# A decoder layer's kernel written anew around other layouts of its input, queries and keys

## The reference

```python
h = rmsnorm(x, norm_w)                              # x: 1024 tokens x 2048, float32
qa, ka, va, ga, qb, kb, vb, gb = split(h @ w_in)    # 1024 1024 1024 1024 1024 128 128 1024
qa, ka = rope(rmsnorm(qa)), rope(rmsnorm(ka))       # per head of 64 columns; 8 heads x 2 maps
p = softmax(causal(qa @ ka.T / 8))                  # two maps per head
oa = (p[map 0] - lam * p[map 1]) @ va               # 8 heads, values 128 wide
ya = rmsnorm(oa, subln_w) * (1 - lam_init) * silu(ga)
qb, kb = rope(rmsnorm(qb)), rope(rmsnorm(kb))       # 16 query heads, 2 key heads
p = softmax([window_128(qb @ kb.T / 8), sink])[..., :-1]
yb = (p @ vb) * silu(gb)
out = x + concat(ya, yb) @ w_out                    # 2048 x 2048
```

## Time and profile before

| | |
|---|---|
| median of three runs | 1878.39 us |
| the profiled execution | 1879.02 us |
| its span in the trace | 1877.2 us |
| TensorE busy | 1807.0 us, 96% |
| DVE, ACT, POOL busy | 59%, 43%, 23% |
| mean granted clock of TensorE | 0.993 |
| HBM traffic | 138.71 MB read, 45.09 MB written |

### The profile page before, as it was taken

How to read it: one execution, slowest core, us unless ns; L and a number is a source line. 1 busy time by engine, 2 the same in 40 slices (tenths; PEclk the granted TensorE clock), 3 DMA queues, 4 the chain that set the end, 5 groups by cost and what they waited for, 6 DMA issues and landing times.

```text
span 1877.2 us, 27880 instructions
## 1 busy us (share of the span) xinstructions
PE 1807.0 (96%) x8920; PEld 1507.0 (80%) x8920; DVE 1109.2 (59%) x2255; ACT 799.8 (43%) x2116; POOL 439.0 (23%) x664
## 2 busy tenths in 40 slices
PE   3899999999999999999999999999999889999999
PEld 3788878888788887888878888888888678788887
DVE  5734465665656657566575666758677866333333
ACT  5411354444544445444444444445444554222221
POOL 6512131322313223131231312313223521000000
PEclk9999999999999999999999999999999889999999
DMA  5122222222222222222222222323323544444445
GB/s 201 36 79 73 84 72 78 78 78 78 71 77 77 77 78 71 85 69 87 68 74 86 73 84 74 105 82 83 109 80 98 189 127 122 162 154 161 142 143 177
DMA packets 256504, 184.97 MB, mean 99 GB/s; under 512 B 31136, under 2 KB 227744, under 8 KB 255392
## 3 DMA queue, kind: packets, MB, share of 16 engines
q1 hardware_dynamic: 254352, 183.85, 32.3%
q10 hardware_dynamic: 2064, 0.01, 0.1%
HBM read 138.71 MB, written 45.09 MB: 98 GB/s over the span
## 4 chain that ended last, share of the span: by engine, by line
PE 79%; DVE 9%; issue 4%; DMA 3%; ACT 2%; POOL 2%; SPq 1%; DVEq 0%; ACTq 0%
PE ps_a L854 19%; PE ps_a L856 19%; PE ps_a L855 19%; PE ps_b L938 3%; PE ps_b L856 3%; PE ps_b L854 3%; PE ps_b L855 3%; PE ps_a L898 2%; DVE stage_rows L1124 2%; DMA qkv_sb<-qkv_a_dram 2%; PE ps_a L897 2%; PE ps_b L953 2%; PE ps_b L891 2%; PE ps_b L984 1%; DVE w_lo_sb L1124 1%
## 5 line engine op out<-in xcount | busy, mean ns | idle before, releaser
L854 PE MATMUL ps_a<-hT_hi,w_hi_sb 128*128 128x512 f32 x1696 | 694.1, 409 | 7.2 <-DVE stage_rows L1208 4.5
L856 PE MATMUL ps_a<-hT_hi,w_lo_sb 128*128 128x512 f32 x1696 | 667.4, 394 | 0.0
L855 PE MATMUL ps_a<-hT_lo,w_hi_sb 128*128 128x512 f32 x1696 | 664.1, 392 | 0.0
L1124 DVE TENSOR_TENSOR w_lo_sb<-w_raw_sb,w_hi_sb 128x512 fp32r<-128x512 f32 (+1 forms) x320 | 228.3, 716 | 272.1 <-ACT w_hi_sb L657 270.1
L856 PEld LDWEIGHTS ps_a<-hT_hi,w_lo_sb 128*128 128x128 f32 x1696 | 320.1, 189 | 71.8
L854 PEld LDWEIGHTS ps_a<-hT_hi,w_hi_sb 128*128 128x128 f32 x1696 | 321.2, 189 | 70.2 <-issue 7.2
L855 PEld LDWEIGHTS ps_a<-hT_lo,w_hi_sb 128*128 128x128 f32 x1696 | 321.8, 190 | 58.5
L657 ACT ACTIVATE w_hi_sb<-w_raw_sb 128x512 fp32r<-128x512 f32 (+1 forms) x320 | 197.8, 620 | 226.4 <-DMA w_raw_sb<-in_w_out 95.0
L817 ACT ACTIVATE expd<-ps_a,neg_max 128x256 f32<-128x256 f32 (+7 forms) x128 | 95.1, 743 | 213.3 <-DVE neg_max L1265 211.4
L749 ACT ACTIVATE attention_parts<-ps_b 128x512 fp32r<-128x512 f32 (+3 forms) x160 | 76.9, 521 | 224.2 <-PE ps_b L938 224.0
L1124 DVE TENSOR_TENSOR ps_a<-ps_a,mask 128x128 f32<-128x128 f32 (+2 forms) x192 | 77.5, 417 | 142.2 <-PE ps_a L898 140.8
(11 more groups left out here) (126 smaller groups left out, 2651.6 us busy)
## 6 DMA issues: line engine op xcount, KB each, us to landing
w_raw_sb<-in_w_in SPq DMA_DIRECT2D x200, 256.0 KB, 3.1
w_raw_sb<-in_w_out SPq DMA_DIRECT2D x104, 256.0 KB, 3.1
qkv_a_dram<-stage_rows SPq DMA_DIRECT2D x48, 256.0 KB, 2.4
qkv_sb<-qkv_a_dram SPq DMA_DIRECT2D x64, 192.0 KB, 3.0
x_raw_sb<-in_x SPq DMA_DIRECT2D x8, 1024.0 KB, 7.6
gates_dram<-stage_rows SPq DMA_DIRECT2D x32, 256.0 KB, 2.7
gate_y<-gates_dram SPq DMA_DIRECT2D x128, 64.0 KB, 2.4
y_dram<-gate_y SPq DMA_DIRECT2D x128, 64.0 KB, 2.3
```

The source lines that it names most:

```text
L854: pe.matmul(dst, a_hi, b_hi, start=start, stop=False)
L855: pe.matmul(dst, a_hi, b_lo, start=False, stop=False)
L856: return pe.matmul(dst, a_lo, b_hi, start=False, stop=stop)
L1124: return dve.tensor_tensor(o, a, b, op)
```

## The change

The program is new; the arithmetic of the projections, of the attention and of the output is the same, with the same three matmuls for each product.

- The host hands over the input twice, as it is and transposed (`in_xT`), and the weights with their columns and rows in the order in which tiles are read. PE transposes no input. Channel block k of xT is 128x1024; ACT scales it by `norm_w` into `hT_hi`, DVE makes `hT_lo`. The token factor 1/rms is left out of it: the sums of squares come from x as it is (`square_rows`), and the factor is applied to values and gates later, and cancels for queries and keys but for EPS, which is scaled with it.
- The first 4 tiles (pairs 0 and 1) are computed together while the input arrives, in 16 units of 24 matmuls. Then the values are computed with tokens as rows, in 48 units of 24 matmuls that are 384 wide. Then come 37 tiles in half quarters: 296 slots of 12 matmuls 128x512. The weight tiles pass through rings of two raw and three split ones.
- Columns of queries and keys are ordered so that a tile holds the first halves of four heads, and its partner the second halves. Each such pair of tiles is normalised and rotated as it lies, in two jobs of 512 tokens: squares (ACT), their sum (POOL), a matmul with a matrix of 1/64 that sums over a head's rows (`sum_squares`, L865 and L866, 52 matmuls in all), Ln and Exp(-0.5 ln) on ACT, a Newton step (DVE), products with the tables (POOL) and with the head (DVE), hi and lo. There are 26 jobs, two of them for the B keys. Queries and keys are stored as hi and lo, and are read in the form in which the scores need them, so a step transposes and splits neither.
- A step of A takes 2 slots for i < 4 and 4 slots for i >= 4; a step of B takes 3 slots. Its parts stand in later slots by the numbers of `Step`.
- Gates are the last 16 tiles. y and gates are stored apart; `prep` reads both back, POOL multiplies, ACT and DVE split. Four of the 32 pieces stand in the last slots, 28 in the first 14 units of the output, two each.
- All code is written out; there is no loop on the chip.

```diff
-            def turn_tile(d, b, n, bank):
-                wait(pe, pp_copied[b], d["T"] + 1)
-                bank_free(n)
-                for r in range(4):
-                    mm = pe.transpose(p_tr[bank][:, r * P:(r + 1) * P], stage[:, b, r * P:(r + 1) * P], ident[:, :])
-                mm.then_inc(sm["tp_done"], 1)
-            def turn_qk(nk, i, it, first):
...
-                for a in range(2 if nk == "A" else 3):
-                    mm = pe.transpose(bank[:, a * P:(a + 1) * P], qkv[:, i % 2, a * P:(a + 1) * P], ident[:, :])
+def stage_slots(j):
+    pr, d = divmod(j, 2)
...
+    e = 8 * pair_tiles(pr)[1] + 6 + d + (pr == KB_PAIR)
+    h = e + d
+    return dict(sq=e, hl=h + 1, ss=h + 2, u=h + 3, ln=h + 3, nw=h + 4, p1=h + 5, p2=h + 6, out=h + 7, st=h + 8)
+class Step:
...
+        if self.a:
+            wide = self.i >= 4
+            self.s1 = x + 2 if wide else x
+            self.tp = self.s1 + 2
+            self.pv = self.tp + (2 if wide else 1)
+            self.sq, self.osc, self.to = self.pv + 1, self.pv + 2, self.pv + 3
+            self.after = x + (4 if wide else 2)
+        else:
+            self.tp, self.pv = x + 3, x + 5
+            self.after = x + 3
+            def load_xT(k):
+                wait(sp, x_lo, k - 3)
+                sp.dma_start(xT_sb[k % 4], xT[k * P:(k + 1) * P, :]).then_inc(xT_in[k % 4], 16)
+            def load_rows(r):
+                wait(sp, x_sq, r - 1)
+                sp.dma_start(x_rows[r % 2], x[r * P:(r + 1) * P, :]).then_inc(xr_in[r % 2], 16)
+            for k in range(4, KT):
+                load_w(k)
+                load_xT(k)
+                if k < 4 + NR:
+                    load_rows(k - 4)
```

On ACT the start, and the part of a job with Ln and Exp:

```diff
+            def split_w(u):
...
+                act.wait_ge(w_in[u % 2], 16 * (u // 2 + 1))
+                wait(act, w_used, u - 2)
+                act.activation(w_hi[:, u % 3, 0:w], w_raw[:, u % 2, 0:w], ACT.Copy).then_inc(w_hi_ready, 1)
+            for k in range(KT):
+                act.wait_ge(xT_in[k % 4], 16 * (k // 4 + 1))
+                act.activation(hT_hi[:, k, :], xT_sb[k % 4], ACT.Copy, scale=pars[:, C_NORM + k:C_NORM + k + 1])\
+                    .then_inc(x_hi, 1)
+                split_w(k)
+                if 6 <= k < 6 + NR:
+                    square_rows(k - 6)
+            def job_ln(j):
+                d = j % 2
+                act.wait_ge(u_ready, j + 1)
+                act.activation(bufY[d], bufX[d], ACT.Ln).then_inc(ln_done, 1)
+                act.wait_ge(ln_done, j + 1)
+                act.activation(bufQ[d], bufY[d], ACT.Exp, scale=-0.5).then_inc(y0_done, 1)
+                act.wait_ge(y0_done, j + 1)
+                act.activation(bufY[d], bufQ[d], ACT.Square).then_inc(y0_sq, 1)
```

On DVE the walk through the slots, in which a new weight tile stands first and the jobs' parts stand behind the attention's, but for `job_u`:

```diff
+            for slot in range(-48, NHS + 1):
+                if slot < 0:
+                    split_w(U_V + slot + 48 + 2)
+                elif slot % 2 == 0 and slot < NHS:
+                    split_w(U_T + slot // 2 + 2)
...
+                for j in jobs_at("u", slot):
+                    job_u(j)
...
+                for j in jobs_at("nw", slot):
+                    job_newton(j)
+                for j in jobs_at("p1", slot):
+                    job_prod1(j)
...
```

On POOL the product of y and gate:

```diff
+            def prep_mul(j):
+                half, k = prep_hk(j)
+                t = slice(half * 512, (half + 1) * 512)
+                pool.wait_ge(y_in[j % 5], 32 * (j // 5 + 1))
+                pool.tensor_tensor(g_ring[j % 5], f(hT_lo[:, k, t]), g_ring[j % 5], ALU.mult).then_inc(y_mul, 1)
```

More of the change, by code:

```diff
@@ new lines, with steps_at @@
+FIRST_HS = 4
+STEPS = []
+for _g in range(AH * NR + NB * NR):
+    STEPS.append(Step(_g, STEPS[-1].after if STEPS else FIRST_HS))
+NS = len(STEPS)
+def steps_at(what, hs):
+    return [st for st in STEPS if {"s0": st.s0, "s1": st.s1, "tp": st.tp, "pv": st.pv, "to": st.to,
+                                   "sq": st.sq, "osc": st.osc}[what] == hs]
+USE = {}
+for _hs in range(NHS + 16):
+    for _st in steps_at("tp", _hs):
+        for _m in range(len(_st.spans)):
+            USE["P", _st.g, _m] = len(USE)
+    for _st in steps_at("to", _hs):
+        USE["O", _st.g] = len(USE)
@@ L702, in evacuate @@
-            def evacuate(d, before, u, it, first):
-                for b in range(2):
-                    wait(act, sm["w_used" if b else "pp_done"], u * 4 + 4 if b else u + 1)
-                    stage_free(before, b, it, first)
-                    if d["turned"]:
-                        act.activation(stage[:, b, :], p_proj[b], ACT.Copy).then_inc(pp_copied[b], 1)
-                    else:
-                        act.activation(stage[:, b, :], p_proj[b], ACT.Tanh, scale=0.5).then_inc(pp_tanh[b], 1)
@@ new lines, in scores_b @@
+            def scores_b(st):
+                g = st.g
+                pe.wait_ge(q_in[g % 2], 32 * (g // 2 + 1))
+                if st.unit == 0 and st.i in (0, 1, 4):
+                    pe.wait_ge(k_in[0][(0, 1, 0, 0, 2)[st.i]], 16 * (AH + 1))
+                if st.unit == 2 and st.i in (0, 3):
+                    pe.wait_ge(kb1_in[st.i // 3], 16)
+                wait(pe, x_done, 2 * g)
+                t0, t1 = max(st.i - 1, 0) * P, (st.i + 1) * P
+                lo = P if st.i == 0 else 0
+                for n in range(4):
+                    q_hi, q_lo = (q_slot(st)[:, (2 * n + m) * P:(2 * n + m + 1) * P] for m in range(2))
+                    dst = p_s_flat[:, n * 256 + lo:n * 256 + 256]
+                    pe.matmul(dst, q_hi, keys[:, t0:t1], start=True, stop=False)
+                    mm = pe.matmul(dst, q_lo, keys[:, t0:t1], start=False, stop=True)
+                    if n % 2:
+                        mm.then_inc(s_done, 1)
@@ L952, in values @@
+            def values(st):
+                pe.wait_ge(tp_free, last_use(st) + 1)
+                wait(pe, o_read, st.g)
+                if st.a:
+                    if st.i in (0, 1, 4):
+                        m = (0, 1, 0, 0, 2)[st.i]
+                        pe.wait_ge(v_in[m], 16 * (1, 3, 4)[m] * (st.unit + 1))
+                    for b in range(st.i + 1):
                         a = slice(b * P, (b + 1) * P)
-                        pe.matmul(p_o[:, 0:2 * P].rearrange("t (c e) -> t c e", c=2), aT_hi[:, a],
-                                  parts[:, 2:4, a], start=b == 0, stop=False)
@@ L1436, in _ @@
+            for u in range(U_O, N_UNITS):
+                split_w(u + 2)
+                for j in prep_items(NHS + u - U_O):
+                    prep_lo(j)
+                g, k = divmod(u - U_O, KT)
+                if k == KT - 1 and g < len(GROUPS) - 1:
                     add_group(g)
@@ new lines, in tile_columns, with halves @@
+def tile_columns():
+    first, second = np.arange(HALF), np.arange(HALF) + HALF
+    def halves(base, rows):
+        heads = base + HD * np.asarray(rows)[:, None]
+        return [(heads + first).reshape(-1), (heads + second).reshape(-1)]
+    start = halves(0, range(4)) + halves(AW, range(4))
+    tiles = []
+    for m in range(1, 4):
+        rows = range(4 * m, 4 * m + 4)
+        tiles += halves(0, rows) + halves(AW, rows)
+    kb = halves(KB0, range(2))
+    tiles.append(np.concatenate(kb))
+    for j in range(NB):
+        tiles += halves(QB0, range(4 * j, 4 * j + 4))
+    tiles += [3 * AW + P * n + np.arange(P) for n in range(8)]
+    tiles += [GB0 + P * n + np.arange(P) for n in range(8)]
+    values = np.concatenate([2 * AW + np.arange(AW), VB0 + np.arange(P)])
+    return np.concatenate(start), values, np.concatenate(tiles)
```

2291 lines of the change are left out of this document (1136 added, 1155 removed).

## The result

The changed kernel takes 2114.5 us (median of 4 runs, 2113.7 to 2115.8), the kernel before 1878.8 (4 runs): ratio 1.126, 95% interval 1.124 to 1.127. The forecast was 1860, its range ended at 1915.

The account below looks back on a forecast made before the run. PE, busy 96% of the span, was taken to bound the kernel. From 1879 us the terms +3 - 59 - 12 + 12 - 17 - 16 + 68 + 2 gave 1860 us, with a range of 1792 to 1915.

Parts of the forecast that it names:

- Products, transposes, sums of squares: PE work: product matmuls +3 us, 528 tile, query and key transposes gone -59, 52 added matmuls for squares +12.
- Start: Input phase: overhead falls from 60 to 43 us, 30 of it waits for x blocks around channel blocks 8 to 12; -17.
- third rival: At the start, x blocks land in time and the loop of waits does not close: -30, 1830 us; chance 8%.
- Small waits: PE's waits for query transposes' loads (7.1 us) and the result's transpose (5.4 us) go: -12, or -7 if the latter stay.
- Seams of the value units: The 48 units that compute the values cost PE +2 us at their seams.
- B steps: Attention steps of B have 11 us for a chain of 7.5 and no jobs beside them: 0 us.
- y pieces: Splitting y: 24 us lost beside attention goes, 8 us of stall comes beside the output's first 14 units; -16.
- Jobs beside the A heads: Norm-and-rotation jobs delay DVE and ACT beside A steps, so PE stalls 6.2 us in each of 11 bursts: +68.
- the signs: If right, A heads show gaps of 1 to 5 us grouped every 16 slots, none between groups or in B steps.
- second rival: Beside A heads, DVE slows beside POOL, bursts cost 11.2 us each: 123 instead of 68, 1915 us; chance 27%.
- The hand chain: One pair followed through slots 16 to 24 beside A heads: 7.4 us of PE stalls, 8.7 over steps i = 2 to 5.
- The first rival: Beside A heads the jobs' lag is absorbed: 15 us instead of 68, 1807 us; chance 20%.

Follow-up runs that it names:

- combo: Changed kernel with one table set for Exp and Ln, job stores split by head, and the result's turn first in its slot: 2013.7 us.
- combo_thin: combo with the jobs' operations on 16 of 512 columns from the second group on, so work is left out: 1886.6 us.

## Why the prediction was wrong

**Products, transposes, sums of squares** (+3 - 59 + 12): right. PE's work fell by 56 us. The forecast had 44, and 14 more are the input's 128 transposes, which it had under the start.

**Start** (-17): right in kind, and 9 us better than forecast. The first matmul starts at 9.2 us (forecast 10) and the four first tiles end at 121.5 us (forecast 125) with 87.3 us of work in them: 34 us of overhead, where the forecast had 43 and the kernel before 60. The gaps stand where the loop of x blocks put them, at channel blocks 8 to 12, with 1.5, 5.1, 4.0, 3.6 and 1.9 us. So the third rival's loop, which does not close, fell too. Two of them:

```profile
67.05 0.80 PE L854 MATMUL ps<-hT_hi,w_hi_sb 128*128 128x512 f32 x1 [4.89 <-DVE w_lo_sb L1058]
...
78.64 0.79 PE L854 MATMUL ps<-hT_hi,w_hi_sb 128*128 128x512 f32 x1 [3.81 <-DVE w_lo_sb L1058]
```

They are 16 us of stalls in all, where I had 30 for the loop; 9 us of lower clock fill part of the difference.

**Small waits** (-12): wrong in the half that counted on the turn's three slots. L949 alone waits 69 us.

**Seams of the value units** (+2): wrong. 29 us of stalls and 10 of clock. Splitting the jobs' stores took 10 of the 29 away; 7.9 are one wait ahead of the first scores, which stays (8.1 with split stores). I had costed the jobs' operations and left out that each job also issues 1 MB of stores into SP's queue, though the diff shows them.

**B steps** (0): right in substance, 11 us of stalls and 4 of clock and restarts in 373.

**y pieces** (-24 + 8): the lag is there, with 26 us and 6 of clock and not 8. My lag was POOL's and DVE's; POOL in fact waits for its loads, 33 us in 1727 to 1817. One of its rows:

```profile
1784.56 2.56 POOL L1480 TENSOR_TENSOR tables<-hT_lo,tables 128x512 f32<-128x512 f32 x2 [2.34 <-DMA tables<-gates_dram]
```

**Jobs beside the A heads** (+68): this is the step that failed, by more than all others together. "I take 6.2 for a burst, 11 x 6.2 = 68" counted the jobs' operations and their table loads. Taken out, the operations gave 133 us with what clock they cost and the loads 30: 163 us in place of 68. The stores, which the step did not have, gave 54 more: 217 us, about 20 a burst. For operations and loads the mechanism was the one forecast (late `lo` parts of probabilities and weights, in-order rows, little loss beside B steps), the size was not; the stores' is another. Of the signs, the stalls did not come in one group for every 16 slots with none between: they stand all over the A heads, up to 11.5 us long, and that with DVE busy for 55% of this stretch, not the 85% that the second rival would have shown. Three things are missing in the step. The hand chain followed one pair from a state without lag and was then cut ("My chain counts each wait at its longest"), where the runs show more, not less. It had no transfers. And it had no clock: beside the A heads 199 us of stalls came with 93 of lower clock and restarts, and over all runs that count goes up and down with the stalls (284 and 124 in the changed kernel, 199 and 111 in combo, 111 and 71 in combo_thin). The forecast even read the row that shows it ("with the clock down behind it") and gave it no price.

**The second rival** had the right sign and the right place. Its mechanism, DVE slowed beside POOL, is real and small; thinning POOL's three long operations gives 43 us in all, slowing and waits together, and DVE's own 50.

**The chances.** The first rival, that the lag is absorbed, had 20% on the ground that the engines are free a quarter of the time. Beside the A heads they are free half of the time in the result (DVE busy 535 of 975 us, ACT 439). Average room says nothing about rows that must be on time within 5.5 us.

## What to carry over

When half as much TensorE work covers the same chain of small operations, count what else comes into the in-order rows at that place: operations, table loads, waits of another task at the head of the row, and the DMAs that the moved work issues: on how many DMA engines their shape puts them, what queues behind them, and which buffers stay taken until they land. Price the stalls with the slow stretches behind them, which here added a third to a half on top (69 to 223 in all, 93 to 199 beside the A heads). And sum the costs by taking work out, not by following one wait: three visible waits were gone after here (turn, POOL's sum, step length). They gave 4 us, -25, and -13 or 32 for two choices of the steps, while the work behind them gave 127.

## What the hardware showed that was not expected

A store of 128 partitions to four heads of 32 rows moved 100 GB/s with the DMA engines two tenths busy, and a 192 KB weight tile behind it took 11.7 us in place of 2.3. The same bytes in four stores, a head each, cost SP 0.59 us an issue and gave back 64 us. A stall of 7.4 us was followed by matmuls 0.43 us apart for 3.1 us before they were 0.23 again.
